# Two transformer layers on one core: order of the first loads, small loads in two groups, the last norm's roots and the output stores

## The chip, the cores and the metric

One NeuronCore of one Trainium2 chip runs the whole program in one launch. The time is device microseconds of the execution. Before the change: a median of 1682.24 us over 3 runs (1681.89 to 1682.55).

## The reference

512 tokens of width 1024 (float32) pass through two layers.

```python
h = rmsnorm(x, mix_pre_g); proj = h @ w_in      # 7 blocks of 1024 columns and 8 forget logits
y_a = gated spatial mixing of gelu(u), gelu(v_s)             # chunks of 128 tokens
y_b = forgetting attention, 8 heads of 128, causal
x = x + rmsnorm((sigmoid(g_a) * y_a + sigmoid(g_b) * y_b) @ w_out, mix_post_g)
x = x + rmsnorm((silu(h @ w_gate) * (h @ w_up)) @ w_down, ffn_post_g)   # h = rmsnorm(x, ffn_pre_g)

mod = silu(c) @ mod_w + mod_b                    # 6 vectors: shift, scale, gate, twice
h = rms_norm(x, g_pre_mix) * (1 + scale1) + shift1
x = x + gate1 * rms_norm(merged(short conv, stick-breaking attention, SSD scan of h) @ w_o, g_post_mix)
h2 = rms_norm(x, g_pre_ffn) * (1 + scale2) + shift2
x = x + gate2 * rms_norm((silu(gt) * up) @ w_ffn_out, g_post_ffn)       # gt, up = split(h2 @ w_ffn_in)
```

`rmsnorm(x, g)` is x / sqrt(mean(x*x) + 1e-6) * g over the 1024 columns of a token.

## The kernel before

Every large product is made in float32r with three passes: each operand is split into a rounded part (hi) and its remainder (lo), and TensorE adds hi*hi, hi*lo and lo*hi (`three_passes`, lines 1360 to 1362) over k-tiles of 128 rows, 512 columns wide, into the PSUM banks 0 to 3. Banks 4 to 7 serve transposes and the smaller work.

The weights come as a stream of units of 128x2048 elements, 1 MB each (`STREAM`, `lay_out_stream`). A unit has one of two slots, alternately. SyncE loads it in two DMAs of 512 KB into `raw` (line 426), ScalarE casts `raw` to `w_hi` (line 691) once TensorE has finished the unit before the last, VectorE subtracts to get `w_lo` (line 968), TensorE multiplies. SyncE's `free(n)` waits until VectorE has split the unit two before. All engines run their own program in order; they meet only at semaphores, and a wait holds everything behind it on its engine. Nothing is scheduled at run time.

The order at the start, in which the change works:

- SyncE issues unit 0 (the first 256 query columns), the four x tiles of 128 tokens, the column `gain_1`, unit 1, then `load_small()` with 24 small DMAs (line 497) that share one semaphore `small_in`, then units 2 and 3 and the rest of the stream.
- GpSimd builds seven masks and a few constants, and then for each x tile `root`: one addition (line 586) and a power of -0.5 (line 587), from the sums of squares. Later it makes six pairs of modulation vectors (`mod_pair`, lines 607 to 619) and the roots of every norm.
- ScalarE casts unit 0, squares each tile in two halves (line 697), scales the left half of a tile (`norm_rows`, line 701), then writes `h_hi` from the transposed banks (line 711). It casts unit 1, waits for `small_in` at 16 * 24, casts the eight forget and eight dt columns (`wf`, `wf2`, lines 796 and 797), makes `c_silu` (line 798) and loads another activation table. Only then does it take results of the query units out of the banks and cast the next units.
- VectorE splits unit 0, scales the right half of each tile (line 978), writes `h_lo` (line 988), then waits for `small_in` and for ScalarE's `wf` casts, subtracts them (lines 1092, 1093), and goes on with the split of unit 1.
- TensorE transposes the left halves of the normalised tiles as they come (line 1443), then in `first_tile` alternates between one k-tile of products and the transposes of a later k-tile (line 1435).

`post_norm` runs four times, behind each output projection and each down projection. Per tile of 128 tokens: ScalarE squares the bank (q), VectorE multiplies the bank by the gain row (m, line 1001), GpSimd makes the root (p, lines 586 and 587), VectorE adds y * root to the residual in two halves (x, line 1025). `DVE_STEPS`, `ACT_STEPS` and `POOL_STEPS` fix the order. The fourth one ends the kernel; behind it SyncE stores each tile of 128x1024 with one DMA (line 553) once both halves are added, and waits for all four.

## Time and profile before

| | us |
|---|---|
| median of 3 runs | 1682.24 |
| profiled execution, its own time | 1683.88 |
| its span | 1682.1 |
| TensorE busy | 1624.4 (97%) |
| VectorE busy | 687.7 (41%) |
| ScalarE busy | 525.6 (31%) |
| GpSimd busy | 503.1 (30%) |
| mean granted TensorE clock | 0.98 |

The span runs from the first to the last event on the core; the execution's own time is 1.8 us longer. In the timeline a line gives the start, the duration, the engine, the source line and the operation; brackets give the idle time before it and what ended that. Matmuls are pipelined, so the start-to-start distance tells their cost and not the duration. "SPq" is the issue of a DMA by SyncE. The granted clock is a share of full speed.

### The profile page before, as it was taken

To read this page: it belongs to the slowest core of one execution; us is meant where nothing else is said; L and a number is where in the kernel's file an instruction comes from. 1 tells how busy PE (TensorE), PEld (TensorE's weight loads), DVE (VectorE), ACT (ScalarE), POOL (GpSimd) and SP (SyncE) were. 2 spreads that over 40 slices of the span, in tenths; PEclk is the share of its full clock that TensorE was granted. 3 is DMA by queue.
4 is the path that set the end of the run, shared out by engine and by line. 5 is a ranking of instruction groups with operands and counts; after the bars stand their busy time and mean duration, and the time that the engine had idled before them with its cause. 6 is when DMAs were issued, how large, how long until landed. Compare 5 with 4: busy or idle time off the path is not lost.

```text
span 1682.1 us, 19149 instructions
## 1 busy us (share of the span) xinstructions
PE 1624.4 (97%) x7330; PEld 1305.7 (78%) x7330; DVE 687.7 (41%) x795; ACT 525.6 (31%) x725; POOL 503.1 (30%) x449
## 2 busy tenths in 40 slices
PE   5999999999899999999899999999998999999997
PEld 3878888888678888888676665788886788888886
DVE  3223454447443333322435655464335433333223
ACT  5223323223442222212434453232224422222121
POOL 2770001300287000086202686177003870000000
PEclk9999999999999999999899999999999999999999
DMA  6533112222444333344221232144322443332331
GB/s 167 176 123 100 51 51 76 75 75 76 150 138 138 100 91 88 108 162 139 87 76 39 70 106 88 50 128 148 100 100 77 137 137 99 89 88 97 110 103 50
DMA packets 187687, 170.76 MB, mean 102 GB/s; under 512 B 20592, under 2 KB 159856, under 8 KB 187632
## 3 DMA queue, kind: packets, MB, share of 16 engines
q1 hardware_dynamic: 179568, 144.84, 28.5%
q0 software_dynamic: 8064, 25.20, 4.7%
q8 instruction: 34, 0.56, 0.1%
q14 instruction: 21, 0.17, 0.0%
HBM read 167.91 MB, written 2.10 MB: 101 GB/s over the span
## 4 chain that ended last, share of the span: by engine, by line
PE 92%; DVE 2%; SPq 2%; ACT 1%; POOL 1%; issue 1%; DMA 0%; DVEq 0%; POOLq 0%; ACTq 0%
PE bank L1360 28%; PE bank L1362 27%; PE bank L1361 27%; SPq L497 1%; PE bank L1646 1%; PE bank L1503 1%; PE bank L1519 1%; PE bank L1595 1%; PE bank L1571 1%; POOL inv_rms L587 1%; PE bank L1511 1%; PE bank L1435 0%; ACT y_out L697 0%; DMA d_col<-in_ssm_d 0%; PE bank L1467 0%
## 5 line engine op out<-in xcount | busy, mean ns | idle before, releaser
L1360 PE MATMUL bank<-h_hi,w_hi 128*128 128x512 f32 x1376 | 556.2, 404 | 13.2 <-DVE w_lo L968 6.4
L1361 PE MATMUL bank<-h_lo,w_hi 128*128 128x512 f32 x1376 | 540.9, 393 | 0.0
L1362 PE MATMUL bank<-h_hi,w_lo 128*128 128x512 f32 x1376 | 540.5, 393 | 0.0
L968 DVE TENSOR_TENSOR w_lo<-raw,w_hi 128x2048 fp32r<-128x2048 f32 (+1 forms) x146 | 314.9, 2157 | 352.9 <-ACT w_hi L691 352.8
L691 ACT CAST w_hi<-raw 128x2048 fp32r<-128x2048 f32 (+1 forms) x146 | 250.7, 1717 | 256.8 <-PE bank L1362 252.8
L1360 PEld LDWEIGHTS bank<-h_hi,w_hi 128*128 128x128 f32 x1376 | 261.4, 190 | 81.3 <-issue 20.5
L1362 PEld LDWEIGHTS bank<-h_hi,w_lo 128*128 128x128 f32 x1376 | 261.2, 190 | 55.9
L1361 PEld LDWEIGHTS bank<-h_lo,w_hi 128*128 128x128 f32 x1376 | 261.6, 190 | 53.6 <-issue 1.9
L616 POOL TENSOR_SCALAR mod_raw<-mod_raw,c_silu 128x512 f32<-128x512 f32 x96 | 177.6, 1850 | 43.0 <-DMA mod_raw<-in_mod_w 39.3
L586 POOL TENSOR_SCALAR sq_y<-sq_y 128x1 f32<-128x1 f32 x16 | 8.1, 505 | 518.1 <-ACT y_down L697 324.8
L619 POOL TENSOR_TENSOR mod_acc<-mod_acc,mod_raw 128x512 f32<-128x512 f32 x96 | 142.6, 1485 | 8.2
L1360 PE MATMUL bank<-w_hi,act_hi 128*128 128x512 f32 x352 | 137.5, 391 | 0.0
L1362 PE MATMUL bank<-w_hi,act_lo 128*128 128x512 f32 x352 | 137.0, 389 | 0.0
L1361 PE MATMUL bank<-w_lo,act_hi 128*128 128x512 f32 x352 | 136.9, 389 | 0.0
L1056 DVE TENSOR_TENSOR bank<-bank,silu_t 128x512 f32<-128x512 f32 x44 | 30.8, 700 | 222.8 <-PE bank L1362 222.8
L773 ACT CAST act_hi<-bank 128x512 f32 x44 | 25.8, 587 | 247.9 <-DVE bank L1056 247.9
L1360 PEld LDWEIGHTS bank<-w_hi,act_hi 128*128 128x128 f32 x352 | 66.1, 188 | 13.9 <-issue 0.2
L1362 PEld LDWEIGHTS bank<-w_hi,act_lo 128*128 128x128 f32 x352 | 66.1, 188 | 13.8
L1361 PEld LDWEIGHTS bank<-w_lo,act_hi 128*128 128x128 f32 x352 | 66.1, 188 | 13.8 <-issue 0.2
L607 POOL MEMSET mod_acc<- 128x512 f32 x12 | 6.3, 527 | 206.3 <-PE bank L1467 182.6
L634 POOL TENSOR_SCALAR gate_a<-gate_a 128x512 f32<-128x512 f32 x8 | 12.0, 1495 | 178.9 <-ACT gate_a L750 178.9
L614 POOL DMA_DIRECT2D mod_raw<-in_mod_w x96 | 55.8, 582 | 21.4 <-POOL mod_acc L619 21.4
(276 smaller groups left out, 1756.6 us busy)
## 6 DMA issues: line engine op xcount, KB each, us to landing
raw<-in_w_in SPq DMA_DIRECT2D x102, 512.0 KB, 4.5
mod_raw<-in_mod_w POOLq DMA_DIRECT2D x96, 256.0 KB, 3.1
raw<-in_w_ffn_in SPq DMA_DIRECT2D x44, 512.0 KB, 4.7
raw<-in_w_gate SPq DMA_DIRECT2D x22, 512.0 KB, 4.0
raw<-in_w_up SPq DMA_DIRECT2D x22, 512.0 KB, 5.3
raw<-in_w_down SPq DMA_DIRECT2D x20, 512.0 KB, 4.1
raw<-in_w_ffn_out SPq DMA_DIRECT2D x20, 512.0 KB, 4.2
raw<-in_w_out SPq DMA_DIRECT2D x8, 512.0 KB, 4.4
```

The lines of the kernel that those rows point to most:

```text
L497: sp.dma_start(dst, src).then_inc(small_in, 16)
L587: gp.tensor_tensor(inv_rms[:, t:t + 1], total, power[:], ALU.pow).then_inc(ready, 1)
L614: gp.dma_start(mod_raw[:, ahead % 2, :], mod_w[ahead, :, col:col + 512]).then_inc(mod_w_in[ahead % 2], 16)
L616: then(gp.tensor_scalar(mod_raw[:, s, :], mod_raw[:, s, :], c_silu[:, k:k + 1], None, ALU.mult))
L619: ins = gp.tensor_tensor(acc, acc, mod_raw[:, s, :], ALU.add)
L691: ins = act.copy(w_hi[s][:, cols], raw[s][:, cols])
L773: act.copy(act_hi[:, bass.ds(2 * i + j, 1), :].rearrange("p a n -> p (a n)"), bank[:, 4 + j, :]).then_inc(act_hi_done, 1)
L968: ins = dve.tensor_tensor(w_lo[s][:, cols], raw[s][:, cols], w_hi[s][:, cols].bitcast(F32), ALU.subtract)
L1056: dve.tensor_tensor(bank[:, 4 + j, :], bank[:, up, :], silu_t[:, j, :], ALU.mult).then_inc(emptied[up], 1)
L1360: pe.matmul(o, st_hi, mv_hi, start=first, stop=False)
L1361: pe.matmul(o, st_hi, mv_lo, start=False, stop=False)
L1362: return pe.matmul(o, st_lo, mv_hi, start=False, stop=last)
```

## The change

- SyncE issues the four x tiles first, then `gain_1`, then unit 0 in two halves with a semaphore of its own for the first half, then units 1 and 2, ten small loads, unit 3. The other 14 small loads (`load_small_2`, own semaphore) go between the gate units and the next stage.
- ScalarE squares the x tiles, casts the first half of unit 0, then the second, then writes `h_hi`. VectorE scales both halves of every x tile; it splits the first half of unit 0 ahead of `h_lo` and the second behind `h_lo` 1.
- ScalarE's wait for the (now ten) small loads and what follows it stand behind the take of unit 1; VectorE's subtraction of `wf` stands ahead of the key units.
- GpSimd builds only the identity before the x roots and the other masks behind them. In the last `post_norm` it has no part: ScalarE takes Sqrt of the mean square, VectorE a reciprocal, and refines it by one Newton step in `refine_root`.
- Each half tile of the output is stored by its own DMA as soon as it is added.

```diff
-    raw = [0, 0]
+    raw = [-16, 0]
...
-             "q0 q1 s0 q2 n0 s1 q3 n1 s2 s3 n2 n3", "q0 q1 q2 q3"]
-POOL_STEPS = ["p0 p1 r0 p2 r1 p3 r2 r3", "p0 p1 r0 p2 r1 p3 r2 r3", "p0 p1 r0 p2 r1 p3 r2 r3", "p0 p1 p2 p3"]
+             "q0 q1 s0 q2 n0 s1 q3 n1 s2 s3 n2 n3", "q0 e0 q1 e1 q2 e2 q3 e3"]
+POOL_STEPS = ["p0 p1 r0 p2 r1 p3 r2 r3", "p0 p1 r0 p2 r1 p3 r2 r3", "p0 p1 r0 p2 r1 p3 r2 r3"]
...
-            (gain_2[:], column("ffn_pre_g")), (gain_3[:], column("g_pre_mix_2")), (gain_4[:], column("g_pre_ffn_2")),
-            (sgu_g[:], column("sgu_norm_g")),
             (bias_f[0:HEADS, :], a["b_forget"].rearrange("a h -> h a")),
             (a_log[0:HEADS, :], a["ssm_a_log_2"].rearrange("a h -> h a")),
-            (bias_dt[0:HEADS, :], a["ssm_dt_bias_2"].rearrange("a h -> h a")),
-            (conv_b[:], column("ssm_conv_b_2")), (norm_w[:], column("ssm_norm_w_2")),
             (w_sp[:], a["w_spatial"][0].rearrange("g t s -> t g s")),
             (gain_row[:], a["mix_post_g"][0].partition_broadcast(P)),
             (b_sp[:], a["b_spatial"][0].partition_broadcast(P)),
+            (sgu_g[:], column("sgu_norm_g")), (gain_2[:], column("ffn_pre_g")),
+        ]
+        assert len(loads) == SMALL
+        with nc.allow_non_contiguous_dma(reason="a few thousand scalars, once"):
+            for dst, src in loads:
+                sp.dma_start(dst, src).then_inc(small_in, 16)
+    def load_small_2():
+        loads = [
+            (gain_3[:], column("g_pre_mix_2")), (gain_4[:], column("g_pre_ffn_2")),
+            (bias_dt[0:HEADS, :], a["ssm_dt_bias_2"].rearrange("a h -> h a")),
+            (conv_b[:], column("ssm_conv_b_2")), (norm_w[:], column("ssm_norm_w_2")),
         ]
         for k in range(CONV_K):
...
-    load_f(n_q, w_in, Q_COL)
     for t in range(NT):
         sp.dma_start(x_in[:, t, :], x_v[:, t, :]).then_inc(x_loaded[t], 16)
     with nc.allow_non_contiguous_dma(reason="a few hundred scalars, once"):
         sp.dma_start(gain_1[:], column("mix_pre_g")).then_inc(gain_1_in, 16)
+    r = ktiles(raw[0], 8, 256)
+    sp.dma_start(r[:, 0:4, :], w_in[:, 0:4, Q_COL:Q_COL + 256]).then_inc(raw_first, 16)
+    load(n_q, r[:, 4:8, :], w_in[:, 4:8, Q_COL:Q_COL + 256])
     load_f(n_q + 1, w_in, Q_COL + 256)
+    load_f(n_q + 2, w_in, Q_COL + 512)
     load_small()
-    for j in (2, 3):
-        load_f(n_q + j, w_in, Q_COL + 256 * j)
+    load_f(n_q + 3, w_in, Q_COL + 768)
     stream_f(n_k, w_in, K_COL, 2)
     stream_t(n_va, w_in, VA_COL)
     stream_f(n_g, w_in, GA_COL, 4)
+    load_small_2()
     stream_t(n_vs, w_in, VS_COL)
...
     for t in range(NT):
-        sp.wait_ge(x_added, 8 * 3 + 2 * t + 2)
-        sp.dma_start(out_v[t], x_res[:, t, :]).then_inc(stored, 16)
-    sp.wait_ge(stored, 16 * NT)
+        for half, cols in enumerate(HALVES):
+            sp.wait_ge(x_added, 8 * 3 + 2 * t + half + 1)
+            sp.dma_start(out_v[t][:, cols], x_res[:, t, cols]).then_inc(stored, 16)
+    sp.wait_ge(stored, 32 * NT)
...
+    then(gp.memset(power[:], -0.5))
+    triangle(ident_r, 1.0, 0.0, -1, 1, ALU.is_equal).then_inc(consts, 1)
+    gp.wait_ge(consts, 1)
+    for t in range(NT):
+        gp.wait_ge(x_squared, 2 * t + 2)
+        root(sq_x, t, x_root)
     for t, keep, fill, step, mult, op in (
-            (ident_r, 1.0, 0.0, -1, 1, ALU.is_equal),
...
-    post_norm(3)
...
+        if k == 3:
+            act.preload_act_table(ACT.Sqrt)
...
+            elif what == "e":
+                act.wait_ge(y_squared, 8 * k + NT + t + 1)
+                act.wait_ge(sq_shifted, 1)
+                act.activation(rms_y[:, t:t + 1], sq_y[:, NT + t:NT + t + 1], ACT.Sqrt,
+                               bias=sq_y[:, t:t + 1]).then_inc(y_root, 1)
...
-    split(0)
     for t in range(NT):
         act.wait_ge(x_loaded[t], 16)
         for half, cols in enumerate(HALVES):
             square(xn_1[:, t, cols], x_in[:, t, cols], sq_x[:, NT * half + t:NT * half + t + 1]).then_inc(x_squared, 1)
-        if t > 0:
-            norm_rows(0, x_in, xn_1, t - 1)
-    norm_rows(0, x_in, xn_1, NT - 1)
+    act.wait_ge(raw_first, 16)
+    act.copy(w_hi[0][:, 0:1024], raw[0][:, 0:1024]).then_inc(hi_first, 1)
+    split(0, part=1)
     act.wait_ge(gain_1_in, 16)
     hi_parts(0, gain_1, None)
     split(n_q + 1)
-    act.wait_ge(small_in, 16 * SMALL)
-    act.copy(wf_hi[:], wf[:]).then_inc(wf_split, 1)
-    act.copy(wf2_hi[:], wf2[:]).then_inc(wf_split, 1)
-    act.activation(c_silu[:], c_col[:], ACT.Silu).then_inc(c_ready, 1)
-    act.preload_act_table_set("natural_log_exp_and_others")
-    then(act.activation(a_neg[0:HEADS, :], a_log[0:HEADS, :], ACT.Exp))
     for j in range(4):
         if j > 0:
             split(n_q + j + 1)
         take(n_q + j, 0, q_t[:, 2 * j, :], STILL, ACT.Copy, float(P) ** -0.5)
+        if j == 1:
+            act.wait_ge(small_in, 16 * SMALL)
+            act.copy(wf_hi[:], wf[:]).then_inc(wf_split, 1)
+            act.copy(wf2_hi[:], wf2[:]).then_inc(wf_split, 1)
+            act.activation(c_silu[:], c_col[:], ACT.Silu).then_inc(c_ready, 1)
+            act.preload_act_table_set("natural_log_exp_and_others")
+            then(act.activation(a_neg[0:HEADS, :], a_log[0:HEADS, :], ACT.Exp))
...
+            if k == 2 and after_two is not None:
+                after_two()
...
+    def refine_root(t):
+        total, step, inv = root_tmp[:, 0:1], root_tmp[:, 1:2], inv_rms[:, t:t + 1]
+        dve.wait_ge(sq_shifted, 1)
+        then(dve.tensor_tensor(total, sq_y[:, t:t + 1], sq_y[:, NT + t:NT + t + 1], ALU.add))
+        then(dve.reciprocal(inv, rms_y[:, t:t + 1]))
+        then(dve.scalar_tensor_tensor(step, inv, inv, total, ALU.mult, ALU.mult))
+        then(dve.tensor_scalar(step, step, -0.5, 1.5, ALU.mult, ALU.add))
+        then(dve.tensor_tensor(inv, inv, step, ALU.mult))
...
+        if k == 3:
+            dve.tensor_scalar(sq_y[:, 0:NT], sq_y[:, 0:NT], EPS, None, ALU.add).then_inc(sq_shifted, 1)
...
+                if k == 3:
+                    refine_root(t)
...
-    split(0)
     for t in range(NT):
-        norm_rows(0, x_in, xn_1, t)
+        dve.wait_ge(x_root, t + 1)
+        for cols, ready in zip(HALVES, (xn_a_ready, xn_b_ready)):
+            dve.tensor_scalar(xn_1[:, t, cols], x_in[:, t, cols], inv_rms[:, t:t + 1], None, ALU.mult).then_inc(ready, 1)
+    dve.wait_ge(hi_first, 1)
+    dve.tensor_tensor(w_lo[0][:, 0:1024], raw[0][:, 0:1024], w_hi[0][:, 0:1024].bitcast(F32), ALU.subtract).then_inc(lo_first, 1)
     dve.wait_ge(gain_1_in, 16)
-    lo_parts(0, gain_1, None)
-    dve.wait_ge(small_in, 16 * SMALL)
-    dve.wait_ge(wf_split, 2)
-    dve.tensor_tensor(wf_lo[:], wf[:], wf_hi[:].bitcast(F32), ALU.subtract)
-    dve.tensor_tensor(wf2_lo[:], wf2[:], wf2_hi[:].bitcast(F32), ALU.subtract).then_inc(wf_split, 1)
+    lo_parts(0, gain_1, None, after_two=lambda: split(0, part=1))
     for n0, dst in ((n_q, q_t), (n_k, k_t)):
+        if n0 == n_k:
+            dve.wait_ge(small_in, 16 * SMALL)
+            dve.wait_ge(wf_split, 2)
+            dve.tensor_tensor(wf_lo[:], wf[:], wf_hi[:].bitcast(F32), ALU.subtract)
+            dve.tensor_tensor(wf2_lo[:], wf2[:], wf2_hi[:].bitcast(F32), ALU.subtract).then_inc(wf_split, 1)
...
-        wait(pe, lo_done, n + 1)
+        if n == 0:
+            pe.wait_ge(lo_first, 1)
+        else:
+            wait(pe, lo_done, n + 1)
         wait(pe, emptied[2 * UNITS[n]["half"]], UNITS[n]["round"])
         pe.wait_ge(xn_b_ready, NT * c + NT)
         for k in range(KD):
+            if n == 0 and k == 4:
+                wait(pe, lo_done, 1)
             pe.wait_ge(h_lo_done, KD * c + k + 1)
...
+    pe.wait_ge(consts, 2)
```

## Rows read from the trace of the kernel before

**Rows 1.** The page's chain that ended last, shares of the span by engine.
```profile
PE 92%; DVE 2%; SPq 2%; ACT 1%; POOL 1%; issue 1%; DMA 0%; DVEq 0%; POOLq 0%; ACTq 0%
```

**Rows 2.** Who waited for whom: total us, times, longest; of TensorE.
```profile
PE bank L1360 <- DVE w_lo L968: 6.6, 2, 6.4
```

**Rows 3.** Timeline of the opening: start, us, engine; and one piece of the chain.
```profile
0.81 1.00 SPq L426 DMA_DIRECT2D raw<-in_w_in  x2
...
1.85 2.08 SPq L506 DMA_DIRECT2D x_in<-in_x  x4
...
7.35 0.51 SPq L426
...
17.34 2.42 ACT L711 ACTIVATE h_hi<-bank,gain 128x512 fp32r<-128x512 f32 x4 [0.63 <-PE bank L1443]
...
19.03 0.76 PE L1360 MATMUL bank<-h_hi,w_hi 128*128 128x512 f32 x1 [1.16 <-DVE h_lo L988]
```

**Rows 4.** DMAs to landing, 0 to 60: tile raw, then tile x_in to 20.
```profile
DMA to landing us min/median/max: 3.8/5.0/9.1
...
DMA to landing us min/median/max: 5.7/6.8/8.2
```

**Rows 5.** TensorE before and behind the stall; one window with its granted clock.
```profile
23.22 0.48 PE L1360 MATMUL bank<-h_hi,w_hi 128*128 128x512 f32 x1
...
33.53 0.39 PE L1362 MATMUL bank<-h_hi,w_lo 128*128 128x512 f32 x1
40.29 0.79 PE L1360 MATMUL bank<-h_hi,w_hi 128*128 128x512 f32 x1 [6.37 <-DVE w_lo L968]
...
43.77 0.39 PE L1362 MATMUL bank<-h_hi,w_lo 128*128 128x512 f32 x1
...
49.90 0.39 PE L1362 MATMUL bank<-h_hi,w_lo 128*128 128x512 f32 x1
...
40.30:42.00 1.70, 1.70 (x4) 1.41 (x5) 0.54 (x1) 1.66 (x4) 1.54 (x3) 0.50 0.26 40
```

**Rows 6.** Small loads and the split of unit 1: timeline, then the chain.
```profile
7.91 3.31 SPq L497 DMA_DIRECT2D c_col<-in_c  x1
...
26.36 1.90 ACT L691 CAST w_hi<-raw 128x2048 fp32r<-128x2048 f32 x1
...
29.36 1.38 SPq L497 DMA_DIRECT2D d_col<-in_ssm_d  x2
...
37.18 0.24 ACT L796 CAST wf_hi<-wf 128x64 fp32r<-128x64 f32 x1 [8.93 <-DMA d_col<-in_ssm_d]
...
30.13 7.03 DMA d_col<-in_ssm_d
...
38.00 2.25 DVE w_lo L968
```

**Rows 7.** Table load by line; half cast on ScalarE; dependent short operations on VectorE.
```profile
L764 ACT ACT_TABLE_LOAD x2 | 2.6, 1283 | 0.0
...
169.72 1.04 ACT L691 CAST w_hi<-raw 128x1024 fp32r<-128x1024 f32 x1
...
169.86 0.17 DVE L1128 RECIPROCAL row_inv<-row_sum 128x1 f32<-128x1 f32 x1 [0.53 <-ACT prob L820]
170.06 0.29 DVE L1129 TENSOR_SCALAR prob<-prob,row_inv 128x128 f32<-128x128 f32 x1
```

**Rows 8.** Timeline of the tail; then the stores' time to landing.
```profile
1671.27 0.60 ACT L697 ACTIVATE y_down<-bank 128x512 f32<-128x512 f32 x1 [2.03 <-PE bank L1362]
...
1671.99 0.69 DVE L1001 TENSOR_TENSOR y_down<-bank,gain_row 128x512 f32<-128x512 f32 x1 [0.20 <-ACT y_down L697]
...
1672.44 0.55 POOL L587 TENSOR_TENSOR inv_rms<-sq_y,power 128x1 f32<-128x1 f32 x1
1673.09 1.42 DVE L1025 SCALAR_TENSOR_TENSOR x_res<-y_down,inv_rms,x_res 128x512 f32<-128x512 f32 x2 [0.41 <-POOL inv_rms L587]
...
DMA to landing us min/median/max: 2.6/2.6/2.7
```

More of the change, by code:

```diff
@@ L267, in build @@
         inv_rms = small("inv_rms", NT)
+        rms_y = small("rms_y", NT)
+        root_tmp = small("root_tmp", 2)
         neg_max = small("neg_max", 2)
@@ L493, in load_small @@
                                   a["ssm_d_2"][0].rearrange("(t h) -> h t", h=2)[half].partition_broadcast(64)))
-                assert len(loads) == SMALL
+                assert len(loads) == SMALL_2
                 with nc.allow_non_contiguous_dma(reason="a few thousand scalars, once"):
                     for dst, src in loads:
-                        sp.dma_start(dst, src).then_inc(small_in, 16)
+                        sp.dma_start(dst, src).then_inc(small_2_in, 16)
             def next_gain(name, k):
@@ L562, in _, with triangle, root @@
             then = chain.then
+            def triangle(t, keep, fill, step, mult, op):
+                then(gp.memset(mod_acc[:, 0, 0:P], keep))
+                return gp.affine_select(out=t[:], in_=mod_acc[:, 0, 0:P], compare_op=op, fill=fill, base=0,
+                                        pattern=[[step, P]], channel_multiplier=mult)
+            def root(sq, t, ready):
+                total = sq[:, t:t + 1]
+                then(gp.tensor_scalar(total, total, sq[:, NT + t:NT + t + 1], EPS, ALU.add, ALU.add))
+                gp.tensor_tensor(inv_rms[:, t:t + 1], total, power[:], ALU.pow).then_inc(ready, 1)
+            then(gp.memset(power[:], -0.5))
[4 more added lines that the diff above has]
+                root(sq_x, t, x_root)
             for t, keep, fill, step, mult, op in (
-                    (ident_r, 1.0, 0.0, -1, 1, ALU.is_equal),
                     (mask_qk, 0.0, MASKED, -1, 1, ALU.is_ge),
@@ L572, in _ @@
                     (neg_suffix, -1.0, 0.0, -1, 1, ALU.is_ge)):
-                then(gp.memset(mod_acc[:, 0, 0:P], keep))
-                then(gp.affine_select(out=t[:], in_=mod_acc[:, 0, 0:P], compare_op=op, fill=fill, base=0,
-                                      pattern=[[step, P]], channel_multiplier=mult))
+                then(triangle(t, keep, fill, step, mult, op))
             then(gp.tensor_tensor(head_sel[:], ident[:, 0:HEADS], ident[:, 32:32 + HEADS], ALU.add))
@@ L578, in _ @@
             then(gp.tensor_scalar(neg_ones[:], ones[:], -1.0, None, ALU.mult))
-            then(gp.tensor_scalar(zeros_st[:], ones[:, 0:1], 0.0, None, ALU.mult))
-            gp.memset(power[:], -0.5).then_inc(consts, 1)
-            gp.wait_ge(consts, 1)
-            def root(sq, t, ready):
-                total = sq[:, t:t + 1]
-                then(gp.tensor_scalar(total, total, sq[:, NT + t:NT + t + 1], EPS, ALU.add, ALU.add))
-                gp.tensor_tensor(inv_rms[:, t:t + 1], total, power[:], ALU.pow).then_inc(ready, 1)
+            gp.tensor_scalar(zeros_st[:], ones[:, 0:1], 0.0, None, ALU.mult).then_inc(consts, 1)
+            gp.wait_ge(consts, 2)
             def post_norm(k):
@@ L624, in mod_pair @@
                             gp.wait_ge(mod_summed, m + 1)
-            for t in range(NT):
-                gp.wait_ge(x_squared, 2 * t + 2)
-                root(sq_x, t, x_root)
             gp.wait_ge(c_ready, 1)
@@ L978, in norm_rows, with lo_parts @@
                 dve.tensor_scalar(xn[:, t, 512:], x[:, t, 512:], inv_rms[:, t:t + 1], None, ALU.mult).then_inc(xn_b_ready, 1)
-            def lo_parts(c, gain, shift):
+            def lo_parts(c, gain, shift, after_two=None):
                 if shift is not None:
@@ L1171, in _ @@
             hidden(n_up, 0)
+            dve.wait_ge(small_2_in, 16 * SMALL_2)
             mod_columns(1, gain_3, True)
```

8 lines of the change are left out of this document (5 added, 3 removed).

## Prediction

> **What bounds the kernel now.** Read the chain that ended last first [rows 1]: TensorE holds 92% of it. Nothing that only eases another engine can pay. What can pay is the remainder: where TensorE stands still or runs at its lower clock. The list of who waited for whom [rows 2] has one long stall of TensorE on the split weights, 6.4 us. The timeline places it [rows 5, 6]: TensorE issues its last matmul of weight unit 0 at 33.53 and the first of unit 1 at 40.29. The rows before say why. SyncE started issuing the small loads at 7.91; the last of 24 landed 30.13 + 7.03 = 37.16; ScalarE waits for all of them before the two casts at 37.18, VectorE waits for those casts before its split of unit 1, and TensorE for that split. So the stall is a chain of small DMAs placed ahead of a weight split in two in-order engines.
>
> The other two places are the ends. At the start TensorE issues its first real matmul at 19.03 [rows 3]. At the end ScalarE's last square starts at 1671.27, behind the last matmul, and 10.8 us of the span follow [rows 8].
>
> **The opening: x before the weights.** Before, 1 MB of weights is issued at 0.81, and x from 1.85 [rows 3]. The first weight half landed at 0.81 + 3.8 = 4.6, x tile 0, the third 0.5 MB, at 1.85 + 5.7 = 7.55, and x tile 3, the sixth, issued at 3.48 (half a us apart), by 3.5 + 8.2 = 11.7 [rows 3, 4]. That is some 1.4 us per 0.5 MB. With x first its tiles take the first four places: about 4.6, 6.0, 7.4, 8.9. Behind them come the gain column (1,024 elements of 4 bytes, I allow 0.4) and the two halves of weight unit 0: the sixth 0.5 MB ends where x tile 3 ended, plus the column, 12.1.
>
> Two chains now meet at the first matmul.
> - x: the two squares of tile 3 (0.6 each) take 8.9 to 10.2, then GpSimd makes the root as at the end of the kernel, where the power is over 1.1 after the square and its sum (1671.87 to 1672.99) [rows 8]: 11.3. The normalisation moves from ScalarE to VectorE, 0.5 for half a tile; the transposes start at 11.8 and h_hi could start some 0.6 later, 12.4.
> - weights: the second half lands at 12.1, its cast of 128x1024 takes 1.04 [rows 7] and stands ahead of h_hi on ScalarE: 13.15. This is the later one.
> Then h_hi start to first matmul was 19.03 - 17.34 = 1.69 [rows 3]: the matmul comes at 14.8, **4.2 us earlier**. VectorE's first half of w_lo (half of 2.25 [rows 6], 1.2) runs from about 12.0 and ends before; its second half sits between h_lo 1 and 2, where TensorE is still working at the slow pitch on k-tiles 0 and 1 (19.03 to 23.22, 4.2 us for two [rows 3, 5]), so it is hidden. Bounds: if transfers ran without any gap (4.6 + 5 x 1.3 = 11.1) the x chain would decide and the gain is 4.9; if the second half landed like the slowest of the weight halves (7.35 + 9.1 = 16.45 [rows 3, 4]) the gain is nought. The row nearest is x tile 3, the same number of bytes.
>
> **The small loads.** The wait on them moves behind ScalarE's split of unit 2 and its take of unit 1, and VectorE's part behind the four query units. With the first matmul at 14.8, unit 0 ends and unit 1 begins at 14.8 + (33.76 - 19.03) = 29.5. Its split no longer waits: ScalarE's cast of unit 1, at 26.36 before [rows 6], starts 4.2 earlier at 22.2 and takes 1.9; VectorE's 2.25 end at 26.4, 3 us before the need. So 33.76 to 40.29, **6.5 us**, goes. With it goes the lower clock behind the stall: the granted clock there is 0.50 (1.2 GHz of 2.4) and the pitch of matmuls 0.43 instead of 0.227 (27 of them from 43.77 to 49.90) [rows 5]; eight matmuls took 40.29 to 43.77 = 3.48 instead of 1.81, **1.7 us**. What is late next: unit 2's load is now ahead of the small loads but waits for VectorE's split of unit 0 (about 17); it lands near 22 and is needed at 29.5. The ten small loads are issued behind it. 24 took 22.8 us of issue (7.91 to 29.36 + 1.38 [rows 6]), so ten take 9.5, to about 28, and land by 28 + 7 = 35. ScalarE reaches its wait at 29.5 + 5.5 + 0.6 = 35.6. The casts, two table loads of 1.28 [rows 7] and two short activations, some 3.5 us, end at 39.1, before unit 1 ends on TensorE (40.4) and its buffer comes free for unit 3. Unit 3's load, now behind the ten, is issued by 28 and has 12 us. GpSimd's six masks move behind the roots; TensorE needs them only in later stages. GpSimd's first modulation pair begins a little earlier. Fourteen small loads go behind the gate units' loads, in attention. Fourteen at 0.95 are 13 us. SyncE may load a unit as soon as the one two before it is split, and a unit of 48 matmuls lasts at least 10.9 us there, more with a head's own work between them; so a load has a wait before it and a whole unit before its use. I count nothing; with one unit's cover gone it would be 13 - 10.9 = 2 us.
>
> **The tail.** Before, GpSimd made the root, over at 1672.99, while VectorE multiplied by the gain, so VectorE stood still only 0.41 before the last addition at 1673.09 [rows 8]. Now ScalarE takes a Sqrt (hidden, about 0.3 as other short operations, [rows 6]) and VectorE itself does five chained operations on 128x1. A reciprocal of that shape starts at 169.86 and what depends on it at 170.06: 0.20 each [rows 7], five are 1.0; were each as slow as ScalarE's short cast of 128x64 (0.24 and a gap of 0.04 [rows 6]) it would be 1.4. VectorE per tile: 0.62 (start of the multiplication to the next start) + 1.0 + 1.41 = 3.0, while TensorE delivers a tile each 12 matmuls, 12 x 0.227 = 2.72 [rows 5]. Three tiles push the last one back by 3 x 0.3 = 0.85; the last addition starts at 1671.99 + 0.85 + 0.62 + 1.0 = 1674.5, 1.4 later than before. Against this stands the store. The old one, 512 KB, was issued once both additions (1.41) were done and landed 2.6 later [rows 8]. A 256 KB one saves half of the 1.3 to 1.4 us per 0.5 MB of the opening [rows 3, 4]: 0.65. (If all of the 2.6 is fixed, it saves nothing.) The first half goes 0.66 ahead and is out of the way. Sum of the tail **+0.7**, bounds: +1.8 to +2.9 with no gain of the store, the larger with 1.4 per root (four times 0.4 more); -0.6 if the five operations cost nothing on the path.
>
> A rule speaks against this part. The Trainium skill, "ScalarE: Activation LUTs", section "Table sets: the hidden batching unit", says that functions of different sets make a table load at each change, and cheap ones are in every set. Here the Silu load stands at its own line, twice, before the two hidden layers, and the squares of the down projections behind them need none [rows 7]; that Sqrt's set holds Square as well, no row shows. The page's 2.7 us for a load is 1.28 in this trace; by either the added preload lies before the first square, where ScalarE waits for TensorE.
>
> A second rule would turn the tail round: the skill's "VectorE: DVE Perf Modes", section on the TRN2 errata, puts an SBUF operation at 58 cycles plus its elements. That is about 0.06 us for 128x1 at the page's 0.96 GHz (an estimate from that page), five are 0.3 and the tail would come out 0.8 us shorter than before, not 0.7 longer. The trace disagrees with 0.16 us for the reciprocal, so the sum goes by the trace.
>
> **Sum.** 4.2 + 6.5 + 1.7 - 0.7 = 11.7 us less. TensorE is the chain from 43.8 to 1671 and every load in between is released by work of the same chain, so I expect the shift to arrive whole. The profiled execution took 1683.88 (span 1682.1 and 1.8 around it): 1672.2. The median of the runs shown, 1682.24, is 1.6 lower: **1670.5**.
>
> **Rivals.**
> - *The wait moves* (6%). If ten small loads still need the 29.25 us from 7.91 to 37.16, they land at about 47; ScalarE then splits unit 3 at 50.5 and VectorE ends at 54.7 while TensorE wants it at 51.3: 3.4 lost and 1.7 of clock, 1675.6. For it: each tiny load has an issue of its own; against: 14 are fewer, and the depthwise weights in small columns are among those moved away.
> - *Weights late in the opening* (9%): the far bound above, no gain from the reordering, 1674.7. It needs the weight half to land 4 us behind the bytes' own pace.
> - *Table loads in the tail* (3%). Were Square and Sqrt in different sets, ScalarE would need 0.7 + 0.3 + 2 x 1.28 = 3.56 per tile against 2.72; the last root comes at 1677.3 and the addition at 1678.2, 3.7 later: 1674.2.
> - *The tail as short as before or shorter* (7%): small operations that overlap on VectorE, the tail -0.6: 1669.2.
> - *Slower* (3%). Matmuls come earlier but keep the slow pitch: in the opening it lasted until 23.2, though TensorE had been at work since 19.0 [rows 3, 5]. Each matmul at 0.43 costs 0.2 us, so 58 such matmuls beyond today's opening eat the whole 11.7, and it decides from there; units 0 and 1 have 96, all of them low give 1670.5 + 18.3 = 1688.8. Against: behind the stall the fast pitch came back after 3.5 us of matmuls, in the opening after 4.2.
>
> My forecast's own case has 72%. Under 0.2% (3.4 us) this measurement cannot tell a change from none. All cases but the slow one and mixtures of several mishaps lie beyond that: faster 0.94, within 0.03, slower 0.03. The range is 1667.5 to 1674.5: down to an opening at its best (-0.7), a short tail (-1.3) and the 0.7 by which runs differ; up to a tail of +1.8, a loss of some 2 us in the opening and the same 0.7 (the sum of the bounds would be wider; not all come together).
>
> **What would show it.** First h_lo matmul near 14.8 and ScalarE's second half cast just before h_hi; no pause between units 0 and 1 and the pitch of 0.227 from about 19 on; the c_silu activation with its table load at 36 to 39 without a wait; five small VectorE operations per tile with a pitch of 0.2 and the multiplication of the last tile some 0.8 late; eight stores of 256 KB. Wrong would be: a pause of TensorE at about 51, one before 29.5 + 10.9, or a last addition less than 3 us behind the last matmul's end.

## The result and the profile after

The changed kernel takes **1665.01 us** (median of 4 runs, 1664.70 to 1665.44); the kernel before, run beside it, 1682.07 (1680.71 to 1682.55). The ratio is 0.9903, 95% interval 0.9891 to 0.9916: faster by 17.1 us where 11.7 were forecast, and below the range that was given. The profiled execution took 1665.06 with a span of 1663.3.

The waits of TensorE between 10 and 60 us: engine, line and what it waited for, total us, times, longest. The stall of [rows 2] is gone, and nothing took its place.
```profile
PE bank L1409 <- DVE h_lo L1017: 1.9, 1, 1.9
PE bank L1492 <- DVE xn L1132: 1.4, 2, 0.9
```

The opening, timeline: start, us, engine, line, operation (answers to [rows 3]).
```profile
0.80 1.82 SPq L519 DMA_DIRECT2D x_in<-in_x  x4
...
3.23 1.13 SPq L523 DMA_DIRECT2D raw<-in_w_in  x1
...
4.16 0.63 ACT L718 ACTIVATE xn<-x_in 128x512 f32<-128x512 f32 x1 [2.08 <-DMA x_in<-in_x]
...
11.30 1.04 ACT L816 CAST w_hi<-raw 128x1024 fp32r<-128x1024 f32 x1 [0.69 <-DMA raw<-in_w_in]
...
12.80 1.05 ACT L712 CAST w_hi<-raw 128x1024 fp32r<-128x1024 f32 x1 [0.46 <-DMA raw<-in_w_in]
13.76 2.41 ACT L732 ACTIVATE h_hi<-bank,gain 128x512 fp32r<-128x512 f32 x4
...
15.44 0.77 PE L1409 MATMUL bank<-h_hi,w_hi 128*128 128x512 f32 x1 [1.86 <-DVE h_lo L1017]
...
20.70 0.63 PE L1411 MATMUL bank<-h_hi,w_lo 128*128 128x512 f32 x1
21.13 0.69 PE L1484 MATMUL bank<-ident,xn 128*128 128x128 f32 x4
21.57 0.48 PE L1409 MATMUL bank<-h_hi,w_hi 128*128 128x512 f32 x1
```
The last thing ScalarE waits for is the second weight half, as the forecast had it, 0.7 later than it said (12.80 against 12.1). The first matmul comes at 15.44, 3.6 earlier than before. TensorE then works at the slow pitch (0.63 for a 128x512) up to 21.13.

The small loads and weight unit 1, timeline (answers to [rows 6]), then a window: PE, PEld, DVE, ACT, POOL busy, granted clock, DMA share, GB/s (answers to [rows 5]).
```profile
18.14 0.51 SPq L492 DMA_DIRECT2D c_col<-in_c  x1
...
23.58 1.90 ACT L712 CAST w_hi<-raw 128x2048 fp32r<-128x2048 f32 x1
...
25.27 1.20 SPq L492 DMA_DIRECT2D gain<-in_ffn_pre_g  x1
25.51 2.29 DVE L995 TENSOR_TENSOR w_lo<-raw,w_hi 128x2048 fp32r<-128x2048 f32 x1 [1.04 <-ACT w_hi L712]
...
37.13 0.24 ACT L828 CAST wf_hi<-wf 128x64 fp32r<-128x64 f32 x1
...
22.00:45.00 23.00, 23.00 (x105) 19.03 (x104) 8.36 (x7) 11.31 (x13) 3.51 (x5) 1.00 0.71 186
```
Unit 1's split ends at 27.8 and TensorE needs it at 31.0; the cast that waited 8.93 us for small loads now starts at 37.13 without a wait; TensorE is busy for the whole of 22 to 45 at a granted clock of 1.00.

The tail, timeline (answers to [rows 8]), and the stores' time to landing.
```profile
1655.88 0.60 ACT L718 ACTIVATE y_down<-bank 128x512 f32<-128x512 f32 x1 [1.70 <-PE bank L1411]
1656.38 0.19 ACT L718 ACTIVATION_READ_ACCUMULATOR y_down<-bank 128x1 f32 x1
1656.61 0.30 ACT L762 ACTIVATE rms_y<-sq_y 128x1 f32<-128x1 f32 x1
...
1657.70 0.69 DVE L1041 TENSOR_TENSOR y_down<-bank,gain_row 128x512 f32<-128x512 f32 x1
1658.42 0.16 DVE L1031 TENSOR_TENSOR root_tmp<-sq_y 128x1 f32<-128x1 f32 x1
1658.62 0.16 DVE L1032 RECIPROCAL inv_rms<-rms_y 128x1 f32<-128x1 f32 x1
...
1659.26 0.16 DVE L1035 TENSOR_TENSOR inv_rms<-inv_rms,root_tmp 128x1 f32<-128x1 f32 x1
1659.45 1.41 DVE L1069 SCALAR_TENSOR_TENSOR x_res<-y_down,inv_rms,x_res 128x512 f32<-128x512 f32 x2
...
DMA to landing us min/median/max: 2.0/2.0/2.1
```
The last addition is *later* behind the last square than before, 3.57 us instead of 1.82. But the span ends 7.4 behind that square and not 10.8. The closing instructions of the program show why. Every engine's program ends with an instruction called DRAIN. Each row is an engine's queue, the operation, its ns, and its start. First the kernel before:
```profile
L133 POOLq EVENT_SEMAPHORE  x2: 17/17/17, 1681.9 to 1682.0; - x2
L133 PEldq DRAIN  x1: 4028/4028/4028, 1667.3 to 1667.3; - x1
...
L133 POOLq DRAIN  x1: 9496/9496/9496, 1672.4 to 1672.4; - x1
L133 DVEq DRAIN  x1: 1397/1397/1397, 1673.2 to 1673.2; - x1
...
L133 SPq DRAIN  x1: 7/7/7, 1677.3 to 1677.3; - x1
```
After:
```profile
L134 POOLq EVENT_SEMAPHORE  x2: 17/17/17, 1663.1 to 1663.2; - x2
...
L134 POOLq DRAIN  x1: 8883/8883/8883, 1367.2 to 1367.2; - x1
...
L134 SPq DRAIN  x1: 7/7/7, 1663.1 to 1663.1; - x1
```
A DRAIN's record can begin while its engine still works. VectorE's ends at 1674.56, 0.05 behind its last addition, and that of TensorE's weight queue at 1671.28, 0.05 behind the last matmul: they only cover work. GpSimd's differs: it began with its last power, which was over at 1672.99, and ended 8.9 us after that; SyncE, with the output stored, was done 4.6 us ahead of it. After, GpSimd closes at 1367 and nothing but the last store is left at the end.

**Where the 18.8 us between the two spans came from**, by the start of the same matmul or square in both traces: 2.8 up to the end of unit 0; 8.2 at unit 1 (it starts at 31.0 instead of 40.29, and with the slow pitch behind the stall gone too, the work at 60 us comes 11.0 earlier); 4.4 in the middle, where the shift grows to 15.4 at the last square; 3.4 behind it. Most of the step of the middle, 3.1, stands at one place. Windows of TensorE, kernel before:
```profile
1078.00:1085.00 7.00, 7.00 (x19) 5.61 (x20) 4.02 (x10) 0.33 (x1) 3.67 (x1) 0.52 0.41 126
```
and the same work after:
```profile
1060.00:1080.00 20.00, 20.00 (x115) 17.41 (x113) 9.62 (x19) 5.61 (x7) 3.66 (x1) 1.00 0.29 92
```
Fourteen 128x512 matmuls ran at the slow pitch there before and none after: 14 x 0.2 = 2.8 us. TensorE was busy throughout in both, and no instruction there was changed.

### The profile page after: what moved, and what is told of

It reads as the page before. It is cut to its first block, busy times and chain, and to the rows that moved or that the text cites. A ratio compares the mean times of both kernels' runs of the same rounds, so it can differ in the third digit from the quotient of the medians.

```text
span 1663.3 us, 19180 instructions
## 1 busy us (share of the span) xinstructions
PE 1618.5 (97%) x7330; PEld 1302.0 (78%) x7330; DVE 688.0 (41%) x821; ACT 525.6 (32%) x727; POOL 501.3 (30%) x441
## 4 chain that ended last, share of the span: by engine, by line
PE 94%; DVE 2%; ACT 1%; POOL 1%; issue 1%; DMA 1%; SPq 0%; DVEq 0%; ACTq 0%
PE bank L1409 28%; PE bank L1411 28%; PE bank L1410 28%; PE bank L1701 1%; PE bank L1558 1%; PE bank L1574 1%; PE bank L1626 1%; PE bank L1650 1%; POOL inv_rms L592 1%; PE bank L1566 1%; DMA raw<-in_w_in 1%; PE bank L1484 0%; PE bank L1521 0%; ACT y_out L718 0%; PE bank L1689 0%
## 5 line engine op out<-in xcount | busy, mean ns | idle before, releaser
L995 DVE TENSOR_TENSOR w_lo<-raw,w_hi 128x2048 fp32r<-128x2048 f32 (+1 forms) x146 | 310.4, 2127 | 346.3 <-ACT w_hi L712 346.1
L644 POOL TENSOR_TENSOR mod_acc<-mod_acc,mod_raw 128x512 f32<-128x512 f32 x96 | 146.1, 1522 | 8.2
```

Of the source, the lines that this page charges most:

```text
L644: ins = gp.tensor_tensor(acc, acc, mod_raw[:, s, :], ALU.add)
L995: ins = dve.tensor_tensor(w_lo[s][:, cols], raw[s][:, cols], w_hi[s][:, cols].bitcast(F32), ALU.subtract)
```

## Experiments

Times are medians; "before" is the kernel before in the same job. They ran in four jobs, on chips 12, 4, 12 and 8, in which the kernel before had medians of 1681.0 to 1682.3. The changed kernel was in none of the first three, so a difference from it compares two jobs, with mostly four runs on each side that can lie 5 us apart. What a part is worth is therefore read from the traces as well.

**gp_root: the last norm's roots back on GpSimd, half-row stores kept.**
```
-  "q0 e0 q1 e1 q2 e2 q3 e3"]        # ScalarE: square, Sqrt
+  "q0 q1 q2 q3"]
+  POOL_STEPS ... "p0 p1 p2 p3"];  post_norm(3) on GpSimd; no refine_root
```


> The changed kernel with only the last norm's roots put back on GpSimd (half-row stores kept). Theory D (the end is set by GpSimd: after its last instruction it runs a closing DRAIN of about 9.5 us, and the program ends at the later of that and the landing of the last store): GpSimd's last power starts about 1.2 us after the last square, at 1657.05, and the span ends 9.6 later at 1666.7, 3.4 longer than the changed kernel: 1668.4 us. Rival S (the stores by halves brought the short end, GpSimd has nothing to do with it): the additions come 1.7 us earlier than with VectorE's refinement and the end follows the landing: 1663.3 us.

Measured: 1668.59 (1667.15 to 1671.11), ratio 0.9928 (0.9911 to 0.9945), profiled 1668.09.
```profile
1657.32 1.41 DVE L1064 SCALAR_TENSOR_TENSOR x_res<-y_down,inv_rms,x_res 128x512 f32<-128x512 f32 x2 [0.41 <-POOL inv_rms L592]
...
L134 POOLq DRAIN  x1: 9499/9499/9499, 1656.6 to 1656.6; - x1
...
L134 SPq DRAIN  x1: 7/7/7, 1661.0 to 1661.0; - x1
```
The last addition comes early again (1.81 behind the last square at 1655.51), the output is stored by 1661.0, and the program still ends at 1666.4, with the drain. By the arithmetic and the stores alone the old roots would be the faster ones.

**late_gp: the changed kernel with one tiny GpSimd operation behind the last addition.**
```
+ gp.wait_ge(x_added, 8 * 3 + 2 * NT)
+ gp.memset(power[:], 0.0).then_inc(late, 1);  gp.wait_ge(late, 1)
```


> The changed kernel plus one GpSimd memset of 128x1 behind the last addition; nothing reads it. Theory D: the closing DRAIN starts at about 1661.0 instead of 1367 and takes about 9.2: the span grows by 6.8, 1671.8 us. Rival S, or any theory in which only the stores count: no change, 1665.0 us.

Measured: 1672.78 (1670.09 to 1672.88), 7.8 above the changed kernel for an instruction of 0.1 us. In the traces 7.1 of it stand behind the last square (14.5 us to the end of the span, against 7.4).
```profile
1661.69 0.10 POOL L696 MEMSET power<- 128x1 f32 x1 [293.91 <-DVE x_res L1072]
...
L134 POOLq DRAIN  x1: 8883/8883/8883, 1662.0 to 1662.0; - x1
...
L134 SPq DRAIN  x1: 7/7/7, 1663.8 to 1663.8; - x1
```
Together the two show it: with a power last (gp_root, over at 1657.22) the span ends 9.1 us behind it, with a memset last (over at 1661.79) 9.3 us, whenever the stores land.

**half_stores_only: the kernel before, stored by half rows.**
```
- sp.wait_ge(x_added, 8 * 3 + 2 * t + 2);  sp.dma_start(out_v[t], x_res[:, t, :])
+ for half, cols in enumerate(HALVES):
+     sp.wait_ge(x_added, 8 * 3 + 2 * t + half + 1);  sp.dma_start(out_v[t][:, cols], x_res[:, t, cols])
```

> The kernel before with the output stored by half rows and nothing else. Theory D (the closing drain on GpSimd, 9.5 us from its last power at 1672.4 us, sets the end, not the last store): no change, 1681.5 +- 1; the trace ends with that drain at 1681.9 or so, while the last transfer has landed 0.6 us earlier than the 1677.1 before. Rival (the last store sets the end): 0.6 us less, and a span that ends with the store's landing.

Measured: 1681.69 (ten runs, 1678.74 to 1683.86) against 1681.08, ratio 0.9998 (0.9988 to 1.0007). In its trace SyncE's DRAIN comes at 1676.7 instead of 1677.3, GpSimd's again at 1672.4 and lasts 9494 ns, and the span is the same 1682.1: the 0.6 us is won and hidden.

**after_whole_stores: the changed kernel with 512 KB stores.** (The same lines, exchanged the other way.)

> The changed kernel with the output stored by whole 512 KB row tiles again. With GpSimd's closing drain over at 1376 us the last store sets the end: theory D says the last store lands 2.6 us instead of 2.0 behind the last addition, so 1665.6, with the span's end 0.4 us behind that landing; give or take the slow-pitch matmuls (0.2 us each against 67). Rival (something else of 5 us sets the end in both): unchanged at 1665.0.

Measured: 1668.04 (1664.27 to 1668.20). Its stores land in 2.6 us where the changed kernel's take 2.0, and SyncE's DRAIN stands 4.3 behind VectorE's (1662.0 to 1666.3), which begins with the last additions, against 3.6 (1659.5 to 1663.1). So the store decides now, by some 0.6; the total is 3.0 above 1665.01, and the rest is in the middle (below).

**one_reciprocal: the root as the plain reciprocal of the square root.** It leaves out the refinement step.
```
-  dve.wait_ge(sq_shifted, 1);  total = sq_y[t] + sq_y[NT + t]
   inv = 1 / rms_y[t]
-  step = inv * inv * total;  step = -0.5 * step + 1.5;  inv = inv * step
```


> The changed kernel with the last norm's root taken as the plain reciprocal of ScalarE's square root: the refinement step of VectorE (a sum, two fused steps and a product, 4 of the 5 small operations per row tile) is left out. Theory V (VectorE's queue sets the last addition: 3.6 us lie between the last square and it, of which 4 x 0.2 us are the last tile's small operations, and the earlier tiles' 12 x 0.2 push the m products behind them): the last addition starts 0.8 to 2.0 us earlier behind the last square, and the time is 1663.0 to 1664.2, give or take the slow-pitch matmuls (0.2 us each against 67). Rival S (ScalarE's squares and square roots set it): under 0.3 us less, 1664.7 to 1665.3.

Measured: 1663.35 (1663.19 to 1663.63), ratio 0.9889 (0.9873 to 0.9906), the lowest median but for the one that is also reordered below.
```profile
1655.95 0.60 ACT L718 ACTIVATE y_down<-bank 128x512 f32<-128x512 f32 x1 [1.70 <-PE bank L1406]
...
1657.39 0.16 DVE L1030 RECIPROCAL inv_rms<-rms_y 128x1 f32<-128x1 f32 x1
1657.59 1.41 DVE L1064 SCALAR_TENSOR_TENSOR x_res<-y_down,inv_rms,x_res 128x512 f32<-128x512 f32 x2
```
The last addition starts 1.64 behind the last square instead of 3.57: 1.9 earlier for four operations left out per tile. VectorE's queue, backlog of the earlier tiles included, set the tail's arithmetic.

**The tail over all traces**, from the start of the last square to the end of the span: 10.85 us in all six kernels whose last roots are on GpSimd, by whole or by half stores; 7.4 in the changed kernel and its variants with the same tail; 14.5 in late_gp, 8.0 in after_whole_stores, 5.5 in the two with the plain reciprocal.

**small_only: the kernel before with the grouping of the small loads alone** (weights first, the last norm's roots on GpSimd, whole stores). GpSimd keeps the changed order of masks and roots; its first matmul at 19.15, against 19.03 before, shows no gain from that.
```
- SMALL = 24
+ SMALL, SMALL_2 = 10, 14      # load_small() behind unit 2's load, load_small_2() behind the gate units'
+ if j == 1: act.wait_ge(small_in, 16 * SMALL) ...     # ScalarE: casts, Silu, Exp; VectorE likewise
```

> The kernel before with the grouping of the small loads alone (x and weights in the old order, whole stores, the last norm's roots on GpSimd). Theory A (the stall in front of weight unit 1 is worth its 6.6 us and the slow-pitch stretch behind it another 1.5, whatever the opening does): 8.1 below the 1681.5 that the runs of the kernel before and of its delayed version average, so 1673.4 +- 1.5; TensorE has no wait above 1 us between 30 and 55 us. Rival B (the gap is only covered when x comes first, because the first group then leaves 4 us earlier): a pause of 2 to 4 us remains in front of unit 1 and the time is 1676 to 1678.

Measured: 1672.70 (1669.25 to 1675.02) against 1681.08, ratio 0.9941 (0.9921 to 0.9961): 8.4 less, 8.1 expected; in the traces the work at 60.1 comes 8.2 earlier. TensorE's only waits from 10 to 60 us are those of the opening:
```profile
PE bank L1482 <- ACT xn L720: 13.5, 3, 12.1
PE bank L1399 <- DVE h_lo L1014: 1.2, 1, 1.2
```

**x_first_only: the kernel before with the opening alone.**
```
- load_f(n_q, w_in, Q_COL)                       # ahead of x
+ sp.dma_start(r[:, 0:4, :], ...).then_inc(raw_first, 16);  load(n_q, r[:, 4:8, :], ...)     # behind x
+ split of unit 0 by halves; all of xn_1 on VectorE; GpSimd's roots ahead of its masks
```

> The kernel before with the opening alone changed (x ahead of the weights, split in halves, identity first on GpSimd); 24 small loads in one group with the waits where they were, whole stores, roots on GpSimd. Theory 1 (parts don't add: the restart of TensorE for unit 1 is fixed in time by the last small load, landed at 37.2, whatever the opening does): 1682.1 us, within 1. Rival (parts add up): 3.6 less, 1678.5 us.

Measured: 1681.18 (ten runs, 1679.67 to 1683.10) against 1681.23, ratio 1.0001 (0.9992 to 1.0011): nothing. The waits of TensorE from 0 to 60, and the restart:
```profile
PE bank L1391 <- DVE w_lo L983: 11.0, 1, 11.0
...
40.90 0.80 PE L1391 MATMUL bank<-h_hi,w_hi 128*128 128x512 f32 x1 [11.04 <-DVE w_lo L983]
```
The earlier start only lengthens the stall, since the 24 small loads land when they did.

**weights_first: the changed kernel with the old opening** (the first two edits above, undone; GpSimd's order kept).

> The changed kernel with the opening alone undone (unit 0 loaded ahead of x, split as a whole, rows scaled half on ScalarE, half on VectorE); small loads, tail and stores as changed. Theory 1 (the opening is worth what the trace shows, first matmul 3.6 us earlier, of which 0.8 was lost again to a longer time at the slow pitch): 2.8 to 3.6 us slower, 1668.2 us, give or take 2 for other lengths of the slow-pitch episodes further on. Rival (the gain is in the small loads alone, the opening would have been hidden): within 1 us of 1665.0.

Measured: 1668.97 (1666.02 to 1672.38), ratio 0.9921 (0.9905 to 0.9938), 3.7 above the 1665.25 that is the median of all eight runs of the changed kernel (next paragraphs), across jobs and with runs over 6 us apart. With the stall gone the opening pays; its own trace starts the first matmul at 19.37.

**after_d2, after_d4, after_d7 and before_d4: the same kernels, started later.**
```
+ for n in range(d): gp.memset(mod_raw[:, 0, :], 0.0)     # d = 2, 4, 7
+ sp.wait_ge(held, 1)      # ahead of SyncE's first transfer
```


> The changed kernel with everything started later by two GpSimd fills of a 128x512 tile (about 0.53 us each, and some 0.1 us for the waits: 1.1 to 1.3 us in all); SyncE's first transfer waits for them. The computation is otherwise the same. Theory C (the 0.2 us slow-pitch matmuls of the middle come where the granted clock drops, and where and how often it drops depends on the timing of the whole run, not on an instruction that the change touched): the time is 1665.0 + 1.2 plus or minus 0.2 us for each slow-pitch 128x512 matmul more or fewer than the 67 of the changed kernel's trace, with the count somewhere from 60 to 85, so 1665 to 1670, and the stretches of slow pitch stand elsewhere than in the changed kernel's. Rival W (the 4.45 us of the middle are removed work or a removed wait): exactly 1666.2 +- 0.3, the count at 67 and the same stretches 1.2 us later.

> The changed kernel started later by four such fills (2.1 to 2.3 us). Theory C: 1665.0 + 2.2 plus or minus 0.2 us per slow-pitch matmul of difference, 1666 to 1671, the stretches of slow pitch not simply 2.2 us later. Rival W: 1667.2 +- 0.3, the same stretches 2.2 us later.

> The changed kernel started later by seven such fills (3.7 to 3.9 us). Theory C: 1665.0 + 3.8 plus or minus 0.2 us per slow-pitch matmul of difference, 1667.5 to 1672.5. Rival W: 1668.8 +- 0.3, the same stretches 3.8 us later.

> The kernel before started later by four such fills (2.1 to 2.3 us). Theory C: 1682.07 + 2.2 plus or minus 0.2 us for each slow-pitch matmul more or fewer than the 83 of its own trace; the stretches stand elsewhere, and the one of 14 matmuls near 1080 us can be gone (about -2.8), so 1680 to 1686. Rival W: 1684.3 +- 0.3 with the count at 83 and the stretch near 1080 still there, 2.2 us later.

Measured: after_d2 1667.84 (1665.10 to 1669.38); after_d4 1668.25 (1664.50 to 1669.25); after_d7 1669.57 (1667.89 to 1672.32); before_d4 1683.09 (ten runs, 1680.69 to 1685.47) against 1682.34. The first transposes come 1.6, 2.3 and 4.6 later than undelayed. Added to the medians are 2.8, 3.2 and 4.6 for the changed kernel, 0.75 for the one before, whose first transfers wait for the same four fills as after_d4's. With runs 4 to 5 us apart these sums tell little; the spread itself contradicts rival W, which wants one time to 0.3: after_d4 has runs from 1664.50, below every earlier run of the undelayed kernel, to 1669.25. Nor does the count of slow matmuls stay: of those in `three_passes`, 67, 73 and 66 last 0.6 us or more in the delayed kernels' traces, 64 in the changed kernel's, and 73 in before_d4's against 82. Windows of after_d4, over the work that ran at 1.00 in the changed kernel:
```profile
1067.00:1072.00 5.00, 5.00 (x13) 3.94 (x14) 3.18 (x7) 0.00 (x0) 3.66 (x1) 0.50 0.23 58
1072.00:1080.00 8.00, 8.00 (x36) 6.56 (x35) 0.84 (x5) 0.60 (x1) 0.00 (x0) 0.97 0.27 96
```
The slow stretch is back (twelve matmuls). So it belonged to no instruction that the change touched. The delay isn't needed for it either: a second trace of the unaltered changed kernel has it too (after_again, below). What comes ahead of it is the same in all kernels; here in the changed one, which got through:
```profile
1063.47 0.39 PE L1411 MATMUL bank<-h_hi,w_lo 128*128 128x512 f32 x1
1063.70 3.63 PE L1730 MATMUL bank<-ones,z_t 128*128 128x1 f32 x32
1067.19 0.49 PE L1409 MATMUL bank<-h_hi,w_hi 128*128 128x512 f32 x1
```
TensorE counts as busy there, but with 32 matmuls of one column.

**after_again, narrow_split, reciprocal_split.** The first is the changed kernel unaltered. The second breaks that stretch up, with the same instructions; the third is both this and one_reciprocal (so it leaves out the refinement step too).
```
  for g in range(2):
      for t in range(NT):
          ... matmuls of one column (z_t, ones)
+         if t % 2 == 1 and (g, t) != (1, NT - 1):
+             feature_tile(n_mg + 1, 0, STILL, ks=one k-step)
- gate_unit(n_mg + 1, STILL)
+ feature_tile(n_mg + 1, 0, STILL, ks=range(3, 8));  feature_tile(n_mg + 1, 1, STILL)
```


> The changed kernel once more, unaltered. Theory C (where the granted clock drops varies; the first four runs were on the low side): median 1665.5 to 1667, with single runs from 1664.5 to 1669. Rival (1665.0 is its level): median 1665.0 +- 0.3, no run above 1666.

> The changed kernel with the stretch of 32 one-column matmuls near 1064 us (3.5 us without a wide one) broken up: three wide k-steps (three 128x512 matmuls each) of the next unit's tile are moved between its groups of 8; the same instructions, in another order. Theory N (the granted clock falls behind such stretches, so this one is followed by 7 to 14 slow-pitch matmuls in most runs): no slow-pitch matmul between 1060 and 1080 us, and a median 1.5 to 2 us under that of the unaltered kernel in the same job, with less spread. Rival (the drop comes by chance in time, not behind the narrow stretch): no difference (+-0.5), a slow stretch still there in the trace or near it.

> The same order of the narrow matmuls together with the plain reciprocal in the last norm (the refinement step left out). If the two are independent: 1.7 us for the shorter tail and 1.5 to 2 for the clock below the unaltered kernel of the same job, 1662 to 1663.5; if the first 1663.35 of the plain reciprocal already had the clock's gain by chance: 1663.2 to 1663.8.

Measured against 1681.03: after_again 1665.98 (1661.89 to 1666.52); narrow_split 1665.95 (1662.00 to 1666.95), ratio 0.9910 (0.9893 to 0.9926); reciprocal_split 1662.32 (1661.39 to 1665.32), ratio 0.9890 (0.9873 to 0.9906). The window of after_again:
```profile
1064.00:1070.00 6.00, 6.00 (x19) 5.08 (x19) 2.62 (x4) 0.77 (x1) 3.66 (x1) 0.50 0.09 14
```
and of narrow_split:
```profile
1064.00:1070.00 6.00, 6.00 (x35) 5.20 (x36) 2.37 (x2) 0.31 (x2) 3.37 (x1) 1.00 0.03 3
```
The slow stretch is absent in both split kernels' traces, as theory N had it; but the median gained nothing over after_again (expected 1.5 to 2), with four runs each that spread over 5 us, and the profiled execution of narrow_split was its fastest, so the trace says nothing of the other three. That this stretch provokes the drop is therefore supported, not shown, and that splitting it pays is not shown at all. One run of after_again at 1661.89 went beyond what either of its theories allowed. reciprocal_split has the lowest median of all, at least 0.9% under the kernel before by its interval; it is not told apart from one_reciprocal.

**The middle over all traces.** Worked out from the timelines of TensorE: the time from one and the same matmul (at 60.1 us in the kernel before) to the last one, and the slow 128x512 matmuls (0.6 to 0.8 us) behind the narrow stretch.
```
kernel               middle   slow ones there
before              1610.75        14
half_stores_only    1610.71        13
small_only          1608.29        13
before_d4           1607.76         8
x_first_only        1605.07         0
weights_first       1609.64        10
after_d7            1609.50         7
after_whole_stores  1609.12         7
late_gp             1608.65        10
after_d2            1608.52        13
after_again         1608.38        10
after_d4            1608.10        12
gp_root             1607.98        10
one_reciprocal      1607.83        10
reciprocal_split    1607.40         0
after               1606.32         0
narrow_split        1604.82         0
```
The work of the middle is the same in all, and but for the two split kernels its order too; it takes 1604.8 to 1610.8. The first two traces compared, before and after, happened to be a long and a short one. x_first_only, the kernel before in everything past its opening, had the shortest of the unsplit ones. On average there is hardly a difference: 1608.6 over the four traces of kernels that still have the stall (before, half_stores_only, before_d4, x_first_only), 1608.4 over the eleven unsplit ones without it.

## Why the prediction was wrong, step by step

- **What bounds the kernel, and the stall** (6.5 and 1.7 forecast, 8.2 in the traces, 8.4 by the medians of small_only): right, in mechanism and size. Unit 1's split, the ten loads and the casts at 37.13 came within 2 us of the times worked out. The rival in which the wait moves is out.
- **The opening** (4.2 forecast, 2.8 in the changed kernel's profile, about 4.0 over all traces): right in mechanism, and nearly so in size. In that profile the first matmul came at 15.44 instead of 14.8, as the second weight half landed 0.7 later than the bytes' even pace; then the slow pitch lasted 6.1 us instead of the 4.2 taken over from before, 0.8 more. The second part is chance: in after_again the fast pitch was back at 19.34, in the changed kernel's profile at 21.57. Over the eight undelayed traces with this opening and no stall, the first matmul comes at 14.6 to 15.4 and unit 1 begins at 29.0 to 31.0, on average at 29.8; in small_only, with the old opening, at 33.76. The changed kernel's own profile is the slowest of the eight. The Trainium skill, "TensorE: Matmul & The Clock Gate", section on the clock gate ("the warmup mystery"), says of the count of slow matmuls in the start that the same kernel shows different ones from run to run; this case's traces agree, 4 to 9 in the changed kernel and its variants with the same opening.
- **The tail** (+0.7 forecast, -3.4 measured): this is the step that failed. Its sub-steps were right in sign (last addition 1.75 later, forecast 1.4; store 0.6 shorter, forecast 0.65), but the premise "against this stands the store" was not: the store did not end the program before. Of the 10.8 us behind the last square [rows 8] the forecast explained the first 5.8 (addition and landing, to 1677.1) and put the other 5.0 at no change, without asking what they were. They were the rest of GpSimd's DRAIN, which ends 8.9 us after the last power. With the roots off GpSimd the span ends 0.2 behind SyncE's DRAIN instead of 4.8: -4.6, and with the later addition and the shorter store that makes the -3.4. The question that the forecast left out was what lies between the last landing and the span's end. gp_root, late_gp and half_stores_only show it from three sides.
- **"The shift arrives whole"** (0 forecast for the middle, -4.4 in the two profiles): the forecast took the granted clock of the middle as a constant. It is not, and the 4.4 are mostly no gain of the change: the middles of all traces average the same to 0.2, and the profiled execution of the kernel before, 1683.88, was 2.2 above the median of its 50 runs, 1681.7. All eight runs of the changed kernel have a median of 1665.25: 16.4 less. The two profiles' own terms, 2.8 + 8.2 + 3.4, explain 14.4 of it; with the opening's 4.0 over all traces it is 15.6. The variants with a delay agree roughly: with the shift of the first transposes taken off they average 1665.7 (1667.84 - 1.6, 1668.25 - 2.3, 1669.57 - 4.6), and before_d4 comes to 1680.8: 15.1 apart. Whether the last 0.8 are a real gain (a lower chance of slow stretches) or spread is open.
- **The rule on VectorE's short operations.** The tail's five operations last 0.15 to 0.22 each and stand 0.20 apart, 1.03 in all, as worked out. The estimate from the Trainium skill, "VectorE: DVE Perf Modes", section on the TRN2 errata, was 0.3; the trace disagrees, and the section itself says that its row comes out too short for single operations. Its forecast of a shorter tail came true for another reason.
- **The rule on table loads.** Behind the square ScalarE's Sqrt follows at 1656.61 with no load between. The rival in which Square and Sqrt lie in different sets is out. The Trainium skill, "ScalarE: Activation LUTs", section on table sets, says that cheap functions are in every set; it names relu, copy, identity and abs as such and not Square, so for Square it is this trace that shows it. The forecast set the page's 2.7 us for a load against 1.28 in the trace. The same page of the Trainium skill, section "What ACT_TABLE_LOAD costs", gives 1.28 for the load itself and the rest to a drain; here the Silu activation starts at 38.83, 0.02 behind its load, and no such drain shows.
- **Slower**: the slow pitch did not last; 64 matmuls of `three_passes` last 0.6 us or more in the whole trace, against 82 before.

In sum, over all traces: 4.0 + 8.2 + 3.4 = 15.6 where 11.7 were forecast. The tail's error is 4.1 of that and the opening's 0.2 the other way; what the medians show beyond it, 0.8 over all runs and 1.5 in the first four, is not explained.

## What to carry to other kernels

Read what lies between the last store's landing and the end of the span before costing a tail: the closing instructions of each engine are in the trace, and an engine whose closing drain is long has to get its last work early. Parts of a change that act on one gap don't add: the opening alone gained 0.0, the small loads alone 8.4, and the opening on top of them 3.7. And when two profiles differ by more than the edit explains, look at the granted clock over the unchanged work, and profile the same kernel again, before finding a reason in the edit: the second trace of the changed kernel already had the slow stretch that the first one lacked.

## What the runs showed of the hardware

- GpSimd's closing DRAIN ends 8.9 to 9.1 us after GpSimd's last piece of work, in all 17 traces, be that a power, another operation on two tensors or a memset. (Where it is a power, the record of 9.5 us begins with it.) The closing DRAINs of TensorE's weight queue, VectorE and ScalarE end within 0.06 us of the last work of their own engine; their 4.0, 1.4 and 0.3 to 0.7 us are that work. SyncE's takes 0.007. GpSimd's runs beside other engines' work: starting at 1367 it costs nothing. The Trainium skill, "VectorE: DVE Perf Modes", section "The DRAIN you can't avoid", puts those from the start and end of a program at about 12 ns on all engines; for GpSimd these traces show otherwise.
- Behind 32 matmuls of one column (3.6 to 4.8 us in which TensorE counts as fully busy) 13 of 15 traces show 7 to 14 matmuls at a granted clock near 0.50, the lower of the two levels (1.2 GHz), and two none; with wide matmuls put between, two of two show none.
- A 256 KB store from SyncE lands in 2.0 us, a 512 KB one in 2.6.
